# Layer norms through four PSUM banks, handed to the first product block by block

## The reference

```python
for i in range(DEPTH_2):
    kind, j = i % N_MIXERS, i // N_MIXERS
    h = _rmsnorm(x, norm1[i])
    if kind == 0:
        m = _retention_mixer(h, ret_w_in[j], ret_w_out[j])
    elif kind == 1:
        m = _moba_mixer(h, ...)
    else:
        m = _diff_mixer(h, ...)
    x = x + m
    x = x + _squared_relu_mlp(_rmsnorm(x, norm2[i]), w_up[i], w_down[i])
```

## Time and profile before

| what | value |
|---|---|
| median of 3 runs | 2724.21 us (2710.43, 2724.21, 2724.91) |
| the profiled execution | 2707.92 us, its span 2706.1 us |
| mean granted TensorE clock | 0.969 of 2.4 GHz |
| PE busy, share of the span | 2487.4 us, 92% |
| DVE, ACT, POOL busy | 1673.4, 1317.7, 92.0 us |

### The profile page before, as it was taken

The page is one execution under the profiler, slowest core; times in us unless marked ns, Lnnn a source line. Parts: engine busy times, 40 slices in busy tenths (PEclk is TensorE's granted clock), DMA queues, the critical chain, the costliest instruction groups (busy, mean ns, idle before and its releaser), DMA issues.

```text
span 2706.1 us, 32875 instructions
## 1 busy us (share of the span) xinstructions
PE 2487.4 (92%) x13426; PEld 2129.2 (79%) x13426; DVE 1673.4 (62%) x1486; ACT 1317.7 (49%) x1794; POOL 92.0 (3%) x121
## 2 busy tenths in 40 slices
PE   4988999898888999998999999799997999999999
PEld 3867777787777777777878997689975899887898
DVE  6757888785757777775544555655556555644554
ACT  3544776343545766643444444544445444444443
POOL 1000000010000000000000000000001000000000
PEclk9997999998997999999999999999999999999999
DMA  8713999993624988873535584335542455563553
GB/s 279 247 60 135 339 346 331 338 313 108 237 79 138 324 289 293 303 259 120 192 124 174 183 268 140 125 124 188 188 160 87 140 190 186 162 201 125 171 187 125
DMA packets 231301, 539.89 MB, mean 200 GB/s; under 512 B 21072, under 2 KB 29808, under 8 KB 231152
## 3 DMA queue, kind: packets, MB, share of 16 engines
q1 hardware_dynamic: 208992, 471.82, 50.9%
q0 software_dynamic: 15520, 59.77, 6.2%
q10 hardware_dynamic: 6640, 6.20, 1.2%
HBM read 533.54 MB, written 4.19 MB: 199 GB/s over the span
## 4 chain that ended last, share of the span: by engine, by line
PE 64%; DVE 16%; DMA 8%; ACT 7%; issue 4%; POOL 1%; SPq 1%; ACTq 0%; DVEq 0%
DVE w_low L2067 7%; PE pair L958 6%; PE pair L960 6%; PE Y L1074 6%; PE pair L966 6%; PE Y L1076 6%; PE Y L1084 5%; PE pair L991 4%; PE pair L992 4%; PE pair L997 4%; DMA raw<-in_exp_w_down 4%; ACT w_high L1639 3%; DMA raw<-in_exp_w_gate 2%; PE Y L1346 2%; PE Y L1348 2%
## 5 line engine op out<-in xcount | busy, mean ns | idle before, releaser
L2067 DVE TENSOR_TENSOR w_low<-raw,w_high 128x2048 fp32r<-128x2048 f32 (+3 forms) x456 | 1022.0, 2247 | 624.3 <-ACT w_high L1639 619.7
L1639 ACT ACTIVATE w_high<-raw 128x1024 fp32r<-128x1024 f32 (+3 forms) x912 | 911.0, 1038 | 794.8 <-PE Y L1084 203.4
L958 PE MATMUL pair<-hT_high,w_high 128*128 128x256 f32 x1280 | 315.2, 286 | 14.3 <-DVE hT_low L2123 14.3
L960 PE MATMUL pair<-hT_low,w_high 128*128 128x256 f32 x1280 | 314.6, 285 | 0.0
L958 PEld LDWEIGHTS pair<-hT_high,w_high 128*128 128x128 f32 x1280 | 248.8, 194 | 17.1 <-DVE hT_low L2123 15.8
L991 PE MATMUL pair<-w_high,hT_high 128*128 128x512 f32 (+1 forms) x612 | 241.2, 395 | 14.0 <-DVE hT_low L2123 8.7
L960 PEld LDWEIGHTS pair<-hT_low,w_high 128*128 128x128 f32 x1280 | 248.9, 194 | 0.9
L992 PE MATMUL pair<-w_high,hT_low 128*128 128x512 f32 (+1 forms) x612 | 240.1, 393 | 0.0
L1076 PE MATMUL Y<-w_high,gated_low 128*128 128x512 f32 x528 | 205.8, 390 | 0.0
L1074 PE MATMUL Y<-w_high,gated_high 128*128 128x512 f32 x528 | 205.7, 390 | 0.0
L1346 PE MATMUL Y<-w_high,gated_high 128*128 128x512 f32 x320 | 133.6, 418 | 39.6 <-DVE gated_low L2383 35.0
(11 more groups left out here) (364 smaller groups left out, 3688.1 us busy)
## 6 DMA issues: line engine op xcount, KB each, us to landing
raw<-in_exp_w_gate SPq DMA_DIRECT2D x128, 512.0 KB, 4.7
raw<-in_exp_w_up SPq DMA_DIRECT2D x128, 512.0 KB, 5.1
raw<-in_exp_w_down SPq DMA_DIRECT2D x128, 512.0 KB, 4.9
raw<-in_w_up SPq DMA_DIRECT2D x128, 512.0 KB, 4.7
raw<-in_w_down SPq DMA_DIRECT2D x128, 512.0 KB, 4.4
work<-in_w_mod POOLq DMA_DIRECT2D x48, 1024.0 KB, 7.7
raw<-in_ret_w_in SPq DMA_DIRECT2D x96, 512.0 KB, 4.7
raw<-in_ret_w_out SPq DMA_DIRECT2D x32, 512.0 KB, 4.0
```

The lines of the kernel that those rows point to most:

```text
L958: nc.tensor.matmul(ps[:, f, :], high[:, k, f * P:(f + 1) * P], hT_high[:, kk, :], start=(kk == 0 and f % 2 == 0), stop=False)
L960: nc.tensor.matmul(ps[:, f, :], high[:, k, f * P:(f + 1) * P], hT_low[:, kk, :], start=False, stop=False)
L1639: nc.scalar.activation(w_high[:, s % HIGH, part], raw[:, s % RAW, part], ACT.Copy).then_inc(high_ready, 1)
L2067: V.tensor_tensor(w_low[:, s % HIGH, 0:n], part, w_high[:, s % HIGH, 0:n].bitcast(F32), ALU.subtract).then_inc(low_ready, 1)
```

## The change

The eight late norms of the second stack get a path of their own (`by_block`). They no longer use the pair tensors. PE turns x into Y: depth blocks k and k + 4 share bank k (`norm_ps`). After the first half of x it issues the four transposes of b = 0 for banks 0 and 1; after the second half the other twelve, bank after bank, with an increment of `norm_turned` after each bank. ACT evicts one block at a time, waiting for its bank, and for k >= 4 until DVE is done with block k - 4 of the same bank, and increments `norm_high_made` after each. DVE follows block by block and increments `norm_block_made`. The first product waits for a block where it first reads it (`ready`, `block_ready`). The number and the size of the instructions that move or compute data stay the same. The core of the diff:

```diff
@@ norm_plan
-    n.uses = p.fills(2)
-    n.high = p.take("high", 2)
+    n.by_block = late and not both
+    if n.by_block:
+        n.turn, n.block = p.take("turn", 4), p.take("block", KD)
+    else:
+        n.uses = p.fills(2)
+        n.high = p.take("high", 2)
@@ build
+        norm_ps = [Y[:, 512 * (k % 4) + S * (k // 4):512 * (k % 4) + S * (k // 4 + 1)] for k in range(KD)]
@@ tensor: transposed_product(use, ready=None)
                 for j in range(2):
-                    if j and other_half is not None:
-                        wait_emptied(pe, other_half)
...
                         kk = j * half + k
+                        if f == 0 and ready is not None:
+                            ready(kk)
@@ tensor: token_product(..., block_ready=None)
                         kk = j * half + k
+                        if b == 0 and block_ready is not None:
+                            block_ready(kk)
@@ tensor
+            def norm_by_block(n):
+
+                def turn(b, k):
+                    return nc.tensor.transpose(norm_ps[k][:, b * P:(b + 1) * P], x[:, b, k * P:(k + 1) * P], ident)
+
+                pe.wait_ge(updated, TB * (n.after - 1) + 1)
+                for bank in range(2):
+                    turn(0, bank)
+                    turn(0, bank + 4)
+                pe.wait_ge(updated, TB * n.after)
+                for bank in range(4):
+                    for b in range(TB):
+                        if b or bank >= 2:
+                            turn(b, bank)
+                            last = turn(b, bank + 4)
+                    last.then_inc(norm_turned, 1)
+
+                def ready(k):
+                    pe.wait_ge(norm_block_made, n.block + k + 1)
+                return ready
@@ tensor: mlp, retention, softmax_layer
-                other_half = norm(m.norm)
+                ready = norm_by_block(m.norm)
...
-                        transposed_product(m.up[j], other_half=None if j else other_half)
+                        transposed_product(m.up[j], None if j else ready)
...
-                    token_product(use, other_half=other_half if use is a.proj[0] else None)
+                    token_product(use, block_ready=ready if use is a.proj[0] else None)
@@ scalar
+            def norm_highs(n, g):
+
+                for k in range(KD):
+                    if k < 4:
+                        se.wait_ge(norm_turned, n.turn + k + 1)
+                    else:
+                        se.wait_ge(norm_block_made, n.block + k - 3)
+                    nc.scalar.activation(hT_high[:, k, :], norm_ps[k], ACT.Identity, scale=g[:, k:k + 1]).then_inc(norm_high_made, 1)
@@ vector: norm
+                if n.by_block:
+                    for k in range(KD):
+                        ve.wait_ge(norm_high_made, n.block + k + 1)
+                        V.scalar_tensor_tensor(hT_low[:, k, :], norm_ps[k], g[:, k:k + 1], hT_high[:, k, :].bitcast(F32),
+                                               ALU.mult, ALU.subtract).then_inc(norm_block_made, 1)
+                    feed(n.feed)
+                    return
```

More of the change, by code:

```diff
@@ L607, in build @@
         o_made = sem("o_made")
+        norm_turned = sem("norm_turned")
+        norm_high_made = sem("norm_high_made")
+        norm_block_made = sem("norm_block_made")
         latent_turned = sem("latent_turned")
@@ L942, in wait_low, with transposed_product @@
                 pe.wait_ge(low_ready, s + 1)
-            def transposed_product(use, other_half=None):
+            def transposed_product(use, ready=None):
                 ps = quads(pair(use)[:, :])
@@ L968, in transposed_product, with token_product @@
                     last.then_inc(piece_done, 1)
-            def token_product(use, k_blocks=KD, n=512, other_half=None, inputs=(hT_high, hT_low), k0=0, ready=None):
+            def token_product(use, k_blocks=KD, n=512, other_half=None, inputs=(hT_high, hT_low), k0=0, ready=None, block_ready=None):
                 ps = tokpair(pair(use)[:, :])
@@ L1439, in retention @@
             def retention(r):
-                other_half = norm(r.norm)
+                ready = norm_by_block(r.norm)
                 for c, use in enumerate(r.proj):
                     if c < 4:
-                        transposed_product(use, other_half=None if c else other_half)
+                        transposed_product(use, None if c else ready)
                     else:
@@ L1600, in softmax_layer @@
             def softmax_layer(a, nth, mlp_plan_):
-                other_half = norm(a.norm)
+                ready = norm_by_block(a.norm)
                 for use in a.proj:
-                    token_product(use, other_half=other_half if use is a.proj[0] else None)
+                    token_product(use, block_ready=ready if use is a.proj[0] else None)
                 pe.wait_ge(qk_ready, nth)
@@ L1676, in norm_high @@
                     last.then_inc(hT_high_made, 1)
+            def norm_highs(n, g):
[5 more added lines that the diff above has]
+                    nc.scalar.activation(hT_high[:, k, :], norm_ps[k], ACT.Identity, scale=g[:, k:k + 1]).then_inc(norm_high_made, 1)
             def norm(n, g):
-                norm_high(n, g)
+                (norm_highs if n.by_block else norm_high)(n, g)
                 norm_squares(n, tokpair(qT_area))
```

## The result

| what | before | changed |
|---|---|---|
| median | 2717.32 us (4 runs, 2709.53 to 2724.91) | 2690.84 us (4 runs, 2680.44 to 2695.73) |
| ratio, 95% interval | | 0.9899 [0.9871, 0.9927] |
| profiled execution, span | 2706.1 us | 2693.9 us |
| from ret0's first transpose to the end | 1459.7 us (2706.1 - 1246.39) | 1432.9 us (2693.9 - 1261.05) |

What follows compares the result with a forecast made beforehand. PE, busy 92% of the span, was taken as the bound, pausing 2.53 us at seven norms. Boundaries 16.8, ret0 1.3 and clock 8.1 sum to 26.2 us, giving 2698.0 us from a median of 2724.21; range 2681 to 2707.

Steps and rivals of the forecast that it cites:

- First block: First product at a norm: PE may start 1.56 us after the second batch of transposes starts, 4.06 before.
- Second block: Transposed first products: PE waits 0.15 us for block 1, leaving 2.35 us gain per boundary; token products don't wait, 2.50.
- ret0: The eighth norm, at PE's lower clock: matmul 1.66 us earlier, less 0.35 for half speed, gain 1.3 us.
- Clock: Five 18 us stretches at boundaries with mean clock 0.91: the drops go with the pause, gain 8.1 us.
- Semaphores: Eight increments and waits per engine in place of two: bounds 0 to 1.6 us in all, taken as 0.
- block k+4 behind k: ACT's new wait for DVE's block in the same bank: met early, DVE's block 0 ending +1.46, ACT wanting block 4 +1.9.
- next weights: Third weight piece in mlp0: low part ready at 1465.22, PE reaches it at 1468.4, 3.2 us of slack.
- Sum: All eight norms: 16.8 + 1.3 + 8.1 = 26.2 us gained.
- Rival (a): Clock drops at the boundaries stay or come elsewhere: 2706.1 us, chance 0.12.
- (b): Pieces behind the first product wait for ACT or DVE, taking the gain back: 2716 to 2724 us, chance 0.06.
- (c): Block-by-block hand-over paces the first product, losing from 1.5 us per block; 2753 us at 2 us; chance 0.02.

Runs made afterwards that it cites:

- PE in groups: Changed kernel, but PE waits for depth block 3 before the first product and block 7 before the second piece; ratio to before 0.9944, second stack 1442.9 us.
- DVE in groups: Changed kernel, but DVE waits for four of ACT's high parts before its first and its fifth low part; ratio to before 0.9953, second stack 1442.9 us.
- the repeat: The changed kernel run and profiled again, nothing altered; ratio to before 0.9917, second stack 1432.3 us.
- the filled pause: Kernel before, with eight 128x128 matmuls nobody reads put into PE's pause at the second stack's eight norms; ratio to before 0.9965, second stack 1456.0 us.
- the two kernels with the same boundaries: Changed kernel with PE waiting only at blocks 0, 1, 2, 4 (second stack 1436.8 us), or with DVE splitting the second weight piece behind the norm (1437.2 us).
- split and deferred, again: Repeat of changed kernel with x's second half added in two instructions and the second weight piece split behind the norm; ratio to before 0.9856, second stack 1425.9 us.

## Why the prediction was right

- **First block, +1.56:** measured +1.61. ACT at +0.48 (0.47), DVE at +0.98, PE 0.63 behind DVE's start (0.58). The run with PE in groups gave +2.79 where the same steps give 2.73, the one with DVE in groups +2.71 for 2.65. Each hand-over was read rightly off one timeline.
- **Second block, a stall of 0.15:** about 0.10, in one instruction. The gain per transposed boundary was 2.34 for 2.35, read at mlp1. For token boundaries the first matmul came 2.45 us earlier, for 2.50.
- **ret0, 1.3:** the first matmul came 1.95 us earlier, 1.66 forecast before the clock's 0.35, as it starts while the last transposes are in flight. The clock took 0.5 of it back, and 1.43 are left at the second piece (1.70 in the repeat).
- **Clock, 8.1:** the drops went, all five, and the filled pause shows that they were the pause's. The term was a little oversized: a drop costs 1.49 us in an MLP stage and about 1.6 at moba and diff, not 1.62; 7.7 in all. The prediction took it whole, without a run that showed it; the filled pause came later.
- **Semaphores at 0, block k+4 behind k at 0, next weights with 3.2 us of slack:** no new wait of PE for any of these in the first products. PE's waits for low weights later in moba and diff are the same four, 3.9 us in all, in both kernels; one of 0.2 us is new, 130 us behind mlp0's norm, and isn't there in the repeat.
- **Sum:** 5 x 2.34 + 2 x 2.45 + 1.43 + 3 x 1.49 + 2 x 1.6 = 25.7, measured 26.8 and, in the repeat, 27.4. The rest is the clock within attentions and retentions, which moves by some us from one execution to the next in every kernel here: the two kernels with the same boundaries and a gain of 22.9 and 22.5 lie on the other side of the sum.

Rival (a): no drop stayed at the boundaries, and none came in their place: over the whole second stack the clock was at its lower level for 53 us before and 33 in the changed kernel, of which the five drops are 17. The rule of the page TensorE: Matmul & The Clock Gate (Trainium skill, "Why this matters for your kernels"), that ties a drop to longer pauses than these, would have kept the drops; the filled pause contradicts it, with 1.50 us back at mlp2, and drops came behind pauses of 2.04 us too. The same page's warning ("A second HAM failure mode: psum-queue depth-cycling") on brief pauses while cycling through PSUM banks did not come true: 1.00 at all seven boundaries. Rivals (b) and (c): no new wait of note, and a step of 0.39 us per block.

What the prediction left open was where the 14 to 16 us between executions come from: the first stack. In the thirteen profiles, all with the same first stack, its end (ret0's first transposes) lies anywhere from 1245.41 to 1265.99. PE in the first stack, in the profile of before and in the longest (split and deferred, again):

```profile
0.00:1246.39 1246.39, 1098.23 (x5313) 0.95 0.69 242
0.00:1265.99 1265.99, 1116.69 (x5312) 0.94 0.68 238
```

PE is busy for 18.5 of the 19.6 us more, with the same matmuls, and idle about as long in both (148 and 149 us). In all thirteen its waits for DMAs add up to 16 to 20 us, and its lower clock level to between 114 and 169 us. So the difference is in matmuls that took longer, not in data that came late. The clock is the likely cause, but its share doesn't account for every profile (the filled pause had 138 us at the lower level and the shortest first stack), and no run tests it.

## What to carry to other kernels

Where a tile passes through three engines on its way to the engine that bounds, and that engine stands still meanwhile, hand it on in the smallest piece that the last engine can start with: a group of four at a joint costs three steps of that joint's producer, at each joint by itself. It is enough that the first pieces come singly. Read what the clock does behind such a pause as well; here a pause of 2.5 us cost 2.3 us by itself and in over half of the cases 1.5 more. And measure a change in the part that it touches: a PE-bound stage repeated to 0.03 us where whole runs of one kernel lay 15 to 30 us apart. A sum over parts that the change doesn't touch can agree with a forecast by luck.

## What the runs showed of the hardware

- Behind pauses of PE of 2.04 to 2.57 us between dense stretches the granted clock fell to half for 3.4 us in 14 of 21 cases, behind pauses of 1.18 and 1.26 us in none of 14; which of the equal pauses it hits isn't the same in different executions. One drop costs 1.48 to 1.50 us in an MLP stage.
- Matmuls whose result nobody reads, put into the pause, went with a clock of 1.00 at all seven boundaries. At ret0 before, the clock rose at 1251.0 us, when PE had done sixteen transposes and nothing else since 6.78 us of idle time.
- One semaphore increment and wait per instruction on ACT and DVE, in place of one per four, cost nothing that shows: eight high parts take 3.03 us in both kernels and eight low parts 3.23.
- ACT reading one PSUM bank, DVE another and PE writing a third at the same time slowed none of them: their instructions keep 0.48, 0.48 and 0.27 us.
